# LayerNorm of a conformer branch: GpSimd adds the channel tiles, TensorE forms mean and variance with one product each, one token tile later

## The reference, cut to what matters

```
u = u_a * jax.nn.sigmoid(u_gate)
y = lax.conv_general_dilated(u, conv_w ...) + conv_b        # causal, 31 taps, per channel
yf = y.astype(jnp.float32)
mu = jnp.mean(yf, axis=-1, keepdims=True)                   # over 512 channels
var = jnp.mean(jnp.square(yf - mu), axis=-1, keepdims=True)
yf = (yf - mu) * lax.rsqrt(var + EPS) * ln_g + ln_b
return jax.nn.silu(yf)
```

## Time and profile before

| | |
|---|---|
| runs of the kernel | 1174.48, 1175.84, 1177.95 us, median 1175.84 |
| the profiled execution | 1175.93 us, span 1174.2 us |
| busy share of the span | PE 93%, DVE 80%, ACT 59%, POOL 29% |
| chain of work that ended last | PE 76%, POOL 8%, DVE 7%, ACT 3%, issue 3%, DMA 2% |
| mean granted TensorE clock | 0.963 of full speed |
| the GLA loop | from 218 to 321 us of the span |
| line L1656, mean and variance products | 32 passes, 16 of each |

### The profile page before, as it was taken

The page is one execution under the profiler, slowest core; times in us unless marked ns, Lnnn a source line. Parts: engine busy times, 40 slices in busy tenths (PEclk is TensorE's granted clock), DMA queues, the critical chain, the costliest instruction groups (busy, mean ns, idle before and its releaser), DMA issues.

```text
span 1174.2 us, 14751 instructions
## 1 busy us (share of the span) xinstructions
PE 1088.0 (93%) x5072; PEld 866.1 (74%) x5072; DVE 940.5 (80%) x888; ACT 697.0 (59%) x703; POOL 342.1 (29%) x306
## 2 busy tenths in 40 slices
PE   7999999879789995699999999999999999999954
PEld 5758888657678884478888888888888888888831
DVE  5479996863756656599999999999999999999826
ACT  6575455314632223377777777777777777777612
POOL 0368998311300002311222212212222122222113
PEclk9989999989989997699999999999999999999978
DMA  9421120200311127389999999999999999999646
GB/s 330 113 72 36 37 72 1 72 1 1 126 37 66 61 68 272 142 331 376 358 391 382 371 402 393 379 404 369 375 354 377 375 356 373 373 351 373 237 176 258
DMA packets 68342, 283.00 MB, mean 241 GB/s; under 512 B 11760, under 2 KB 30368, under 8 KB 41424
## 3 DMA queue, kind: packets, MB, share of 16 engines
q1 hardware_dynamic: 54384, 255.95, 58.6%
q0 software_dynamic: 10544, 18.08, 4.3%
q10 hardware_dynamic: 3376, 8.47, 1.8%
HBM read 275.64 MB, written 26.74 MB: 258 GB/s over the span
## 4 chain that ended last, share of the span: by engine, by line
PE 76%; POOL 8%; DVE 7%; ACT 3%; issue 3%; DMA 2%; SPq 0%; POOLq 0%; DVEq 0%; ACTq 0%
PE ps L1854 17%; PE ps L1853 17%; PE ps L1852 17%; POOL acc L602 8%; PE ps L1847 2%; PE ps L1743 2%; PE ps L1745 2%; PE ps L1744 2%; PE ps L1656 1%; PE ps L1869 1%; PE ps L1774 1%; PE ps L1573 1%; PE ps L1577 1%; DVE ps L1132 1%; PE ps L1579 1%
## 5 line engine op out<-in xcount | busy, mean ns | idle before, releaser
L1454 DVE TENSOR_TENSOR w_lo<-raw,w_hi 128x2048 fp32r<-128x2048 f32 x206 | 467.7, 2290 | 53.2 <-ACT w_hi L987 51.5
L987 ACT ACTIVATE w_hi<-raw 128x2048 fp32r<-128x2048 f32 x206 | 392.4, 1921 | 26.8 <-PE ps L1854 26.8
L1852 PE MATMUL ps<-w_hi,xm_hi 128*128 128x512 f32 x560 | 224.8, 401 | 2.6 <-DVE xm_lo L1459 2.5
L1854 PE MATMUL ps<-w_hi,xm_lo 128*128 128x512 f32 x560 | 224.0, 400 | 0.0
L1853 PE MATMUL ps<-w_lo,xm_hi 128*128 128x512 f32 x560 | 223.2, 399 | 0.0
L1852 PEld LDWEIGHTS ps<-w_hi,xm_hi 128*128 128x128 f32 x560 | 106.1, 189 | 27.9 <-DVE xm_lo L1459 3.4
L1853 PEld LDWEIGHTS ps<-w_lo,xm_hi 128*128 128x128 f32 x560 | 106.4, 190 | 25.5
L1854 PEld LDWEIGHTS ps<-w_hi,xm_lo 128*128 128x128 f32 x560 | 106.2, 190 | 23.9
L1852 PE MATMUL ps<-w_hi,hm_hi 128*128 128x512 f32 x280 | 113.0, 404 | 1.8 <-DVE hm_lo L1472 1.5
L1854 PE MATMUL ps<-w_hi,hm_lo 128*128 128x512 f32 x280 | 111.4, 398 | 0.0
L1853 PE MATMUL ps<-w_lo,hm_hi 128*128 128x512 f32 x280 | 110.8, 396 | 0.0
(11 more groups left out here) (307 smaller groups left out, 1900.2 us busy)
## 6 DMA issues: line engine op xcount, KB each, us to landing
raw<-in_expert_w_up_dram SPq DMA_DIRECT2D x70, 1024.0 KB, 7.7
raw<-in_expert_w_gate_dram SPq DMA_DIRECT2D x70, 1024.0 KB, 7.3
raw<-in_expert_w_down_dram SPq DMA_DIRECT2D x70, 1024.0 KB, 7.8
raw<-in_w_in_dram SPq DMA_DIRECT2D x8, 1024.0 KB, 7.0
raw<-expert_rows SPq DMA_DIRECT2D x12, 512.0 KB, 8.4
xa<-in_x_dram SPq DMA_DIRECT2D x8, 512.0 KB, 8.8
raw<-in_w_out_dram SPq DMA_DIRECT2D x4, 1024.0 KB, 6.4
xin<-in_x_dram SPq DMA_DIRECT2D x8, 512.0 KB, 3.2
```

Source lines behind the costliest of these rows:

```text
L987: act.activation(w_hi[:, slot, :], raw[:, r, :], ACT.Copy).then_inc(hi_rdy, 1)
L1454: dve.tensor_tensor(w_lo[:, slot, :], raw[:, r, :], w_hi[:, slot, :].bitcast(F32), ALU.subtract)\
L1852: pe.matmul(dst, x_hi, w_hi[:, s, cols], start=first, stop=False)
L1854: return pe.matmul(dst, x_lo, w_hi[:, s, cols], start=False, stop=stop)
```

## The change

GpSimd adds the four channel tiles of a half into the first tile of `sq[h]`, in two instructions: tiles 0 and 1 with tiles 2 and 3, then the two sums. It does so with `acc` for the mean and with the squares for the variance. TensorE then needs one product for each half and quantity instead of four. The constants `T_MEAN` and `T_VAR` go from 2 and 4 to 3 and 5. On ScalarE the branch's steps move behind `scaled_keys` and `gate_out`; the first output weight and `conv_out(0)` move from tile 6 to tile 7. On VectorE the centring comes one tile after the mean products, and the scaling behind `heads_gated`.

```diff
-        T_MEAN, T_VAR = 2, 4
+        T_MEAN, T_VAR = 3, 5
...
+            def channel_sum(src, h):
+
+                pool.tensor_tensor(sq[h][:, 0:2, :], src[:, 0:2, :], src[:, 2:4, :], ALU.add).then_inc(pair_rdy, 1)
+                n_pair[0] += 1
+                pool.wait_ge(pair_rdy, n_pair[0])
+                pool.tensor_tensor(sq[h][:, 0, :], sq[h][:, 0, :], sq[h][:, 1, :], ALU.add).then_inc(sum_rdy, 1)
+
             pool.wait_ge(late_in, 16 * 5)
             for t in range(NT):
                 gate_scaled(t)
                 if t:
                     head_rms(t - 1)
+                for h in range(HALF):
+                    if t == T_MEAN:
+                        conv_done(pool)
+                        channel_sum(acc[:, :, h * 512:(h + 1) * 512], h)
+                    if t == T_MEAN + 1:
+                        pool.wait_ge(sq_rdy, h + 1)
+                        channel_sum(sq[h][:], h)
...
                     head_squares(t - 1)
+                if t + 1 < NT:
+                    scaled_keys(t + 1)
+                    gate_out(t + 1)
                 if t == T_MEAN + 1:
                     centred_squares(0)
                     centred_squares(1)
-                if t == T_VAR + 1:
+                elif t == T_VAR + 1:
                     deviation(0)
                     deviation(1)
-                if t == NT - 2:
+                elif t == NT - 1:
                     weights_hi("o0", (n_rdy, HALF))
                     conv_out(0)
-                if t == NT - 1:
                     conv_columns(0)
                     weights_hi("o1")
-                if t + 1 < NT:
-                    scaled_keys(t + 1)
-                    gate_out(t + 1)
...
-                if t == T_MEAN:
+                if t == T_MEAN + 1:
                     centred(0)
                     centred(1)
+                if t:
+                    heads_gated(t - 1)
                 if t == T_VAR + 1:
                     scaled(0)
                     scaled(1)
-                if t:
-                    heads_gated(t - 1)
...
-            def channel_mean(src, h, done):
-                for c in range(CT):
-                    last = pe.matmul(ps[:, 6 + h, :], ones_dc[:], src[c], start=(c == 0), stop=(c == CT - 1))
-                last.then_inc(done, 1)
-
             def conv_mean(h):
-                conv_done(pe)
-                channel_mean([acc[:, c, h * 512:(h + 1) * 512] for c in range(CT)], h, mu_ps)
+                pe.wait_ge(sum_rdy, h + 1)
+                pe.matmul(ps[:, 6 + h, :], ones_dc[:], sq[h][:, 0, :], start=True, stop=True).then_inc(mu_ps, 1)
 
             def conv_var(h):
-                pe.wait_ge(sq_rdy, h + 1)
-                channel_mean([sq[h][:, c, :] for c in range(CT)], h, var_ps)
+                pe.wait_ge(sum_rdy, HALF + h + 1)
+                pe.matmul(ps[:, 6 + h, :], ones_dc[:], sq[h][:, 0, :], start=True, stop=True).then_inc(var_ps, 1)
```

More of the change, by code:

```diff
@@ L271, in layer_program @@
         mu_ps, d_rdy, sq_rdy, var_ps = sem("mu_ps"), sem("d_rdy"), sem("sq_rdy"), sem("var_ps")
+        sum_rdy, pair_rdy = sem("sum_rdy"), sem("pair_rdy")
         sd_rdy, n_rdy, c_rdy = sem("sd_rdy"), sem("n_rdy"), sem("c_rdy")
@@ L647, in row_rms @@
                 rms(stat[:, 24 + t:25 + t], stat[:, 32 + t:33 + t], stat[:, 40 + t:41 + t], 1, 1.0 / D, rs_rdy)
+            n_pair = [0]
+            def channel_sum(src, h):
[3 more added lines that the diff above has]
+                pool.tensor_tensor(sq[h][:, 0, :], sq[h][:, 0, :], sq[h][:, 1, :], ALU.add).then_inc(sum_rdy, 1)
             pool.wait_ge(late_in, 16 * 5)
```

## The result

The changed kernel takes 1177.55 us (median of 12 runs, 1176.43 to 1180.42) against 1175.06 us of the kernel before (12 runs beside it, 1173.47 to 1177.95). The ratio is 1.0022, 95% interval 1.0012 to 1.0033: slower by 2.5 us, where 1.3 us less was forecast. The time itself lies inside the predicted range.

The account below looks back on a forecast made before the run. TensorE, busy 93% of the span, was taken as the bound, followed through to the first output product. That product moves -3.6 us, plus 2.3 for the clock: 1175.93 - 1.3 = 1174.6 us, range 1171.0 to 1178.5.

Parts of the forecast that it names:

- chain of waits: Waits from VectorE's last convolution steps through the GLA loop to the first output product, which was to start 3.6 us earlier.
- rival of slowed adds: GpSimd's four channel sums slowed by VectorE to 7.6 us a half: +11.3 us, 1187.2 us; chance 0.09.
- rival of a costlier switch: ScalarE's Silu table switch ahead of the projection costs 2.56 us for 1.28: 1175.9 us, no change; chance 0.08.
- rival that TensorE's gain arrives by itself: TensorE's 13 us from mean and variance passes reach the output projection, starting near 315: 1165 us; chance 0.05.
- the clock's term: Lower TensorE clock behind the two waits for the mean sums, priced at 2.3 us, between 1.65 and 3.1.
- the sum: First output product at 322.7 against 326.33, -3.6 us, plus 2.3 for the clock: -1.3 us, 1174.6 us.
- the upper end of the range: 1178.5 us: clock loss 3.1 for 2.3, another 1.65 behind the 2.3 us pause, and the doubled table load.
- the prediction's prices: Clock-fall costs on TensorE from the old profile: 3.1 us as at 253, 1.65 as at 313, 0 if it holds.

Follow-up runs that it names:

- e5: Changed kernel with 12 and 11 overwritten gate passes filling TensorE's two waits for GpSimd's mean sums; 1173.36 us, 0.9977 of the kernel before.
- e4: Changed kernel with the deviation moved back ahead of the scaled keys among ScalarE's steps of tile 6; 1170.26 us, 0.9962 of the kernel before.
- after: The changed kernel as first measured and profiled, against the kernel before; 1177.55 us, ratio 1.0022.
- e1: The changed kernel itself, unaltered, run and profiled once more; 1177.85 us, 1.0021 of the kernel before.
- e9: Changed kernel with one filler pass ahead of each of the two mean products; 1178.12 us, 1.0026 of the kernel before.
- e6: Changed kernel with centring at the end of tile 3 and squares ahead of tile 4's head squares and scaled keys; 1172.89 us, 0.9976 of before.
- e7: Changed kernel with TensorE alone forming the mean, four products per half, at the end of tile 3; 1172.96 us, 0.9961 of the kernel before.
- e2: Kernel before with the two new semaphores declared and never used; 1176.34 us, 1.0004 of the kernel before.
- e8: Changed kernel with early deviation, early centring and squares, TensorE's own mean, and T_VAR set to 4; 1164.07 us, 0.9893 of the kernel before.

## Why the prediction was wrong

Its chain of waits was right nearly to the end, step by step, counted from the keys of tile 2. In brackets what was forecast, from its times of day less 237.22.

- The convolution ends 18.83 us after the keys of tile 2, where it was 15.85: 2.98 later (3.0).
- A half of GpSimd's sums takes 3.65 us (3.85). The rival of slowed adds falls: 2.35 and 1.26 us where the earlier trace rows have medians of 2.41 and 1.30. It was hardly put to the test, since VectorE was idle beside most of the four sums.
- The pauses are 3.28 and 1.90 us, the second short because the product ahead of it ran slowly (3.6 and 2.95). The keys of tile 4 start at 28.17, with the held clock of e5 at 27.40 (27.5).
- The squares behind the gate's activation cost a pause of 2.03 us (2.3), the variance no wait and 1.7 us (1.7).
- The root's load starts 0.90 us after the keys of tile 7 (0.85), the reciprocal 2.02 later. Silu's load stands in the way with 1.28 us; it starts 0.02 us after the first weight and the activation begins 0.01 us after it (316.98, 317.00, 318.29), so the rival of a costlier switch falls. The Trainium skill ("ScalarE: Activation LUTs", What ACT_TABLE_LOAD costs) adds a drain of 1.38 us; this trace shows none.
- From the keys of tile 7 to the projection 25.54 us (25.2). The rival that TensorE's gain arrives by itself falls by e4: it needed the deviation moved.

At the full clock the changed stretch adds up to 27.40 (e5) + 9.63 (e5) + 13.58 + 9.61 (after) + 25.54 = 85.76 us; forecast were 85.48. Against 89.11 that is the gain of 3.4 us the prediction had as 3.6.

**The step that failed is the clock's term:** "I take 2.3, between the two that happened." It priced one fall, the one behind the two pauses for GpSimd's sums, and put the fall behind the 2.03 us pause at nothing in the sum; 1.65 us for it stood in the upper end of the range only. Measured against 85.76 the loss is 1.6, 4.3 and 4.2 us in three profiles (after, e1, e9). The first fall costs 1.6 us in the first profile and 2.7 in e1 (38.62 and 39.73 against 37.03 from tile 2 to tile 5), so 2.3 was near; in e1 not only the two products but also keys, scores and outputs of tile 4 run at 1.2 GHz. The second fall came in two of the three and costs 1.5 (15.13 against 13.58 for tile 5). The first profile had the smaller first fall and no second one, which was luck: its granted clock was the highest of the 24 runs.

The kernel before shows why this term decides the sign. By the prediction's prices its own two falls cost 3.1 and 1.65 us, and both are in the 89.11. At the full clock in both, the new stretch would be 1.4 us longer than the old (85.76 against 84.36, an estimate): the 24 passes saved are used up by the waits and by the late root. So the whole gain of 3.4 us was the old falls going away, and new falls of 4.2 us more than take it back.

Over all runs the full-clock time lost in the span (span times one less the mean clock) is 44.4 us before and 53.0 after. Not all of these 8.6 us reach the time. Some 3.6 of them lie behind the keys of tile 7, where the clock is 0.74 for 25.54 us in the changed kernel and 0.89 for 27.68 before; there TensorE waits 9.57 and then 6.16 us for VectorE, and the stretch has the same length in all six profiles with the late deviation. Another 3.4 lie ahead of it in e1 (64.48 us at 0.89 against 61.43 at 0.94). The versions of the changed kernel can be set against it, as only the clock and a pause differ: e5, e6 and e7 lose 46.5, 49.4 and 45.5 and have 3.7, 4.6 and 5.0 us less mean span; 2.0 of it in e6 is the pause itself, 1.3 in e7 the earlier mean (26.08 against 27.40 from tile 2 to tile 4).

So the sum should have read: 3.4 less, 4.2 for the clock, +0.8 instead of -1.3. A second term was not in it at all. The prediction held the time outside the span at its 1.7 us; it is 2.6 in the changed kernel (24 runs, none under 2.2; the 61 of before none over 1.8). With that the sum is +1.7 of the +2.5 measured. The remaining 0.8 us I can't place: outside the stretch from tile 2 to the projection single profiles differ by up to 3 us (in three of the changed program the keys of tile 2 start between 236.20 and 238.98 us, and from the projection to the end it is 847.8 to 849.3), too much for three profiles to show it.

Where the 0.9 us outside the span come from stays open. It is not the semaphores (e2), not a few instructions more (e9 has 2.6), and not GpSimd's mean sums or the later tile themselves, since e5 has both and 1.7. It goes with the unfilled waits for these sums (after, e1, e4, e9, and in e6 between 1.7 and 2.9), but the longer pause of the kernel before does not bring it, and e8, with unfilled waits for the sums of the squares, has 1.8.

## What to carry to other kernels

Before work is taken off the busiest engine, ask whether it runs while that engine would wait anyway: sums on GpSimd paid for the squares, which had a tile of time, and cost for the mean, which TensorE stood waiting for. A wait that is cut in two is not cheaper when the clock still falls behind the pieces, as it did here behind 3.28 and 1.57 us; price each pause of a chain separately, at what the worse row shows, and look at several executions before a clock loss is taken from one. When a step of a side engine starts the next phase, keep it ahead of the instruction that waits for the main engine: three lines moved back were worth 7 us.

## What the runs showed of the hardware

- TensorE's granted clock fell to 1.2 GHz behind a pause of 2.03 us in e1, e5, e7 and e9 (tile 5 takes 15.1 to 15.2 us), and behind the same pause in the same place not in the first profile of the changed kernel nor in e4 (13.6). The same program does both.
- Passes whose result nobody reads can pay: 23 of them, about 5.3 us of TensorE's time inside its waits, made the kernel 0.45% faster (0.9977 against 1.0022), where two did nothing (1.0026).
- GpSimd's product of 128x512 took 3.02 us in e4, beside VectorE's product of two SBUF tiles, and 1.26 to 1.30 us in the tiles around it, as the 2.63 us of the earlier trace rows already showed. This agrees with the Trainium skill ("SBUF — State Buffer", Who interferes with whom), by which a VectorE instruction with two inputs in SBUF contends with a GpSimd instruction that reads SBUF. The other half of that rule, no contention where one of VectorE's inputs is in PSUM, was met only briefly: in the profile of the changed kernel VectorE was idle beside most of the channel sums, and the second add of the squares, which shares 1.2 us with VectorE's state update from PSUM, took 2.40 us against 2.34 and 2.35.
